# Attention of a two-layer encoder step: pairs alternate between kinds, transposed blocks are copied first, forget sums stand mid-column, units follow the last column piece

## The reference

```python
q_a, k_a, v_a, logf, q_b, k_b, v_b = _project(a, w_in[l], b_f[l], qn_a[l], kn_a[l], qn_b[l], kn_b[l])
F = jnp.cumsum(logf, axis=1)
y_a = _fox_attention(q_a, k_a, v_a, F, F, pos_p, pos_p)        # score + F[q] - F[k], causal, softmax
y_b = _swa_prompt(q_b, k_b, v_b, sink_l, slopes)               # banded, distance penalty, a sink in the softmax
h_p = _merge(h_p, y_a, y_b, w_out[l])
h_p = _channel(h_p, l, g_ffn, w_gate, w_up, w_down, w_router, b_router, we_gate, we_up, we_down)
```

## Time and profile before

| | us |
|---|---|
| median of 3 runs (1336.8 to 1343.54) | 1336.99 |
| the profiled execution | 1331.89 |
| its span | 1330.1 |
| PE busy in the span | 1244.0 (94%) |
| DVE busy | 845.2 (64%) |
| ACT busy | 645.8 (49%) |
| POOL busy | 262.4 (20%) |
| mean granted TensorE clock | 0.904 of full |

### The profile page before, as it was taken

How to read it: one execution, slowest core, us unless ns; L and a number is a source line. 1 busy time by engine, 2 the same in 40 slices (tenths; PEclk the granted TensorE clock), 3 DMA queues, 4 the chain that set the end, 5 groups by cost and what they waited for, 6 DMA issues and landing times.

```text
span 1330.1 us, 20704 instructions
## 1 busy us (share of the span) xinstructions
PE 1244.0 (94%) x7482; PEld 1101.7 (83%) x7482; DVE 845.2 (64%) x1232; ACT 645.8 (49%) x1051; POOL 262.4 (20%) x272
## 2 busy tenths in 40 slices
PE   6998999999999998999997888996999999999993
PEld 6995555579999998999995444886999999999993
DVE  5597444337555654343488553354988988988884
ACT  4533433324232332232433543344788788888871
POOL 3333232212000000111343432120012012012000
PEclk9997556579999998999998987897999999999997
DMA  6541014213333343332531034155999999999984
GB/s 252 209 129 37 1 44 154 102 35 111 126 127 114 123 140 113 117 118 87 212 124 51 1 128 169 51 197 171 363 382 353 378 386 350 379 383 359 370 321 153
DMA packets 58320, 246.72 MB, mean 185 GB/s; under 512 B 7390, under 2 KB 11054, under 8 KB 56208
## 3 DMA queue, kind: packets, MB, share of 16 engines
q1 hardware_dynamic: 53200, 232.78, 48.4%
q0 software_dynamic: 4192, 11.52, 2.3%
q10 hardware_dynamic: 864, 1.57, 0.3%
HBM read 235.22 MB, written 11.68 MB: 186 GB/s over the span
## 4 chain that ended last, share of the span: by engine, by line
PE 81%; ACT 5%; DVE 5%; DMA 4%; issue 3%; POOL 1%; SPq 0%; ACTq 0%; POOLq 0%; DVEq 0%
PE bank L707 21%; PE bank L709 21%; PE bank L708 21%; PE bank L805 4%; PE bank L784 3%; ACT WH L451 3%; PE bank L752 3%; DMA nf_pmt<-nf_rows 2%; DVE WL L457 2%; PE bank L820 2%; PE bank L772 1%; PE bank L768 1%; PE bank L866 1%; PE bank L814 1%; DVE rs L1356 1%
## 5 line engine op out<-in xcount | busy, mean ns | idle before, releaser
L457 DVE TENSOR_TENSOR WL<-raw,WH 128x1024 fp32r<-128x1024 f32 (+3 forms) x206 | 300.0, 1456 | 157.6 <-ACT WH L451 154.9
L451 ACT ACTIVATE WH<-raw 128x1024 fp32r<-128x1024 f32 (+3 forms) x206 | 254.3, 1234 | 286.8 <-PE bank L709 285.7
L707 PE MATMUL bank<-aH,WH 128*128 128x400 f32 (+1 forms) x688 | 246.4, 358 | 3.8 <-DVE aL L1452 1.9
L708 PE MATMUL bank<-aL,WH 128*128 128x400 f32 (+1 forms) x688 | 238.8, 347 | 0.0
L709 PE MATMUL bank<-aH,WL 128*128 128x400 f32 (+1 forms) x688 | 238.6, 347 | 0.0
L707 PE MATMUL bank<-WH,xTH 128*128 128x352 f32 x512 | 168.6, 329 | 3.8 <-DVE WL L457 1.9
L457 DVE TENSOR_TENSOR WL<-raw_more,WH 128x1408 fp32r<-128x1408 f32 (+2 forms) x96 | 156.5, 1644 | 22.4 <-ACT WH L451 21.4
L709 PE MATMUL bank<-WH,xTL 128*128 128x352 f32 x512 | 165.9, 324 | 0.0
L708 PE MATMUL bank<-WL,xTH 128*128 128x352 f32 x512 | 165.8, 324 | 0.0
L451 ACT ACTIVATE WH<-raw_more 128x1408 fp32r<-128x1408 f32 (+2 forms) x96 | 133.6, 1401 | 30.2 <-PE bank L709 29.5
L707 PEld LDWEIGHTS bank<-aH,WH 128*128 128x128 f32 x688 | 130.5, 190 | 9.0 <-DVE aL L1452 2.5
(11 more groups left out here) (208 smaller groups left out, 2099.6 us busy)
## 6 DMA issues: line engine op xcount, KB each, us to landing
raw<-w_egu SPq DMA_DIRECT2D x64, 704.0 KB, 5.9
raw_more<-w_egu SPq DMA_DIRECT2D x64, 704.0 KB, 6.1
raw<-w_gu SPq DMA_DIRECT2D x44, 512.0 KB, 3.5
raw_more<-w_ed SPq DMA_DIRECT2D x24, 768.0 KB, 6.1
raw<-w_ed SPq DMA_DIRECT2D x24, 640.0 KB, 6.6
raw<-w_col SPq DMA_DIRECT2D x26, 512.0 KB, 3.8
raw<-w_d SPq DMA_DIRECT2D x16, 704.0 KB, 4.1
kc<-ck_fox SPq DMA_DIRECT2D x8, 1024.0 KB, 7.4
```

The lines of the kernel that those rows point to most:

```text
L451: nc.scalar.activation(WH[:, p % SPL, 0:w], landing(p), ACT.Copy).then_inc(hi_ready, 1)
L457: nc.vector.tensor_tensor(WL[:, p % SPL, 0:w], landing(p), WH[:, p % SPL, 0:w].bitcast(F32), ALU.subtract).then_inc(lo_ready, 1)
L707: mm(out, aw[0], bw[0], start=start, stop=False)
L708: mm(out, aw[0], bw[1], start=False, stop=False)
```

## The change

Seven things change together:

- `unit_plan` takes the pair as the outer loop and the kind as the inner one: swa 0, fox 0, swa 1, fox 1, and so on. `pair_tile` and the waits of SP's loads follow.
- `COLS` is `[8, 9, 0, 4, 10, 1, 5, 11, 2, 6, 12, 3, 7]`: the swa key and query of pair 0 come first, the fox query and key of pair 3 last.
- The forget sums are formed after piece `XNF` = 4, DVE copies them behind column 4, and SP stores them after it has issued piece 9. The small term moves to the end of `prob`.
- Units follow the last piece: PE scores units 0 and 1 before the last head mean, units 2 and 3 as the banks of the last two roots come free, and the first transpose waits for all columns. ACT takes the last root, and DVE the last column, at step 2.
- POOL handles the last two columns after it has scaled unit 3.
- ACT does `copy_T(i-4)` ahead of `exps(i)`, and copies whole 128-key blocks in one instruction, the left-over one too.
- Scores go to banks 6, 2, 5 and 4 in turn.

```diff
-        for kind in ("swa", "fox"):
-            for pr in range(NPAIR):
+        for pr in range(NPAIR):
+            for kind in ("swa", "fox"):
...
-        eps_ms = nf_smp[:, :, :].rearrange("p s k -> p (s k)")[:, 0:T]
+        eps_ms = prob[:, :, :].rearrange("p n k -> p (n k)")[:, 4 * 384 - T:]
...
+                    if x == XNF + 5:
+                        sp.wait_ge(nf_copied, 2 * l + 2)
+                        sp.dma_start(nf_rows[l], NFp[l][0:H, :]).then_inc(nf_stored, 16)
+                        sp.dma_start(nf_seqs[l], NFs[l][0:64, :]).then_inc(nf_stored, 16)
...
+                for j, u in enumerate(BY_LAYER[l]):
+                    if j == 4:
+                        pool.wait_ge(norm_ready, u["n"])
+                        finish(NCOL - 2)
+                        finish(NCOL - 1)
+                        pool.wait_ge(qbd_ready, 8 * (l + 1))
...
+                    if x == XNF:
+                        pe.wait_ge(em_ready, l + 1)
+                        forget_sums()
...
-                pe.wait_ge(nf_copied, 2 * (l + 1))
-                pe.wait_ge(col_done, (l + 1) * NCOL)
                 for i in range(NU + LAG + 1):
+                    if i == 0:
+                        pe.wait_ge(nf_copied, 2 * (l + 1))
+                    elif i == 1:
+                        pe.wait_ge(col_done, l * NCOL + NCOL - 2)
+                    elif i in (2, 3):
+                        pe.wait_ge(colroot_ready, l * NCOL + NCOL - 3 + i)
+                    elif i == LAG:
+                        pe.wait_ge(col_done, (l + 1) * NCOL)
                     if i < NU:
                         scores(units[i])
+                    if i == 1:
+                        head_mean(NCOL - 1)
...
                 for i in range(NU + LAG + 2):
+                    if i == 2:
+                        head_root(NCOL - 1)
+                    if LAG <= i < NU + LAG:
+                        copy_T(units[i - LAG])
                     if i < NU:
                         exps(units[i])
-                    if LAG <= i < NU + LAG:
-                        copy_T(units[i - LAG])
...
+                    if i == 2:
+                        column(NCOL - 1)
                     if new:
                         add_bias(new)
```

More of the change, by code:

```diff
@@ L191 @@
 NCOL = NPAIR * 3 + 1
-COLS = [0, 4, 1, 5, 2, 6, 3, 7, 8, 9, 10, 11, 12]
+COLS = [8, 9, 0, 4, 10, 1, 5, 11, 2, 6, 12, 3, 7]
+XNF = 4
 CBODY = 6
@@ L620, in add_eps, with finish @@
                     nc.gpsimd.tensor_tensor(sq[:, i % 2, :], sq[:, i % 2, :], eps_ms, ALU.add).then_inc(sqe_ready, 1)
-                add_eps(0)
-                add_eps(1)
-                for x, c in enumerate(COLS):
-                    if x + 2 < NCOL:
-                        if x and (COLS[x - 1] < 4 or COLS[x - 1] > 8):
-                            pool.wait_ge(qbd_ready, 8 * l + sum(y < 4 or y > 8 for y in COLS[:x]))
-                        add_eps(x + 2)
-                    pool.wait_ge(sqe_ready, l * NCOL + min(x + 3, NCOL))
+                def finish(x):
+                    c = COLS[x]
                     pool.wait_ge(col_done, l * NCOL + x + 1)
@@ L642, in _ @@
                         pool.dma_start(o_kswa[l], qk[l][:, c, :]).then_inc(out_done, 16)
-                pool.wait_ge(qbd_ready, 8 * (l + 1))
-                for u in BY_LAYER[l]:
+                add_eps(0)
+                add_eps(1)
+                for x, c in enumerate(COLS):
+                    if x + 2 < NCOL:
+                        if x and (COLS[x - 1] < 4 or COLS[x - 1] > 8):
+                            pool.wait_ge(qbd_ready, 8 * l + sum(y < 4 or y > 8 for y in COLS[:x]))
+                        add_eps(x + 2)
+                    pool.wait_ge(sqe_ready, l * NCOL + min(x + 3, NCOL))
+                    if x < NCOL - 2:
+                        finish(x)
+                pool.wait_ge(sqe_ready, (l + 1) * NCOL)
+                pool.wait_ge(qbd_ready, 8 * l + sum(y < 4 or y > 8 for y in COLS[:-2]))
+                for j, u in enumerate(BY_LAYER[l]):
[4 more added lines that the diff above has]
+                        pool.wait_ge(qbd_ready, 8 * (l + 1))
                     n, rows, keys = u["n"], u["rows"], u["keys"]
@@ L766, in scores @@
                         pe.wait_ge(swc_loaded, 32 * (l + 1))
-                    pe.wait_ge(qbd_ready, l * 8 + d + 1)
+                    pe.wait_ge(qbd_ready, l * 8 + sum(c < 4 or c > 8 for c in COLS[:COLS.index(qc) + 1]))
                     mm(S[:, past:past + P], qbd[l][:, d, 128 * s:128 * s + 128], qk[l][:, kk, TP:T], start=True, stop=True)
@@ L856, in _, with forget_sums @@
                     last.then_inc(piece_done, 1)
+                def forget_sums():
+                    pe.wait_ge(logf_ready, l + 1)
+                    pe.wait_ge(va_copied, 4 * (l + 1))
+                    for i, (t0, r) in enumerate(QT[:3]):
+                        last = mm(bank[6][0:H, 0:TP], lf[0:r, i, :], negtri[0:r, TRI - t0:TRI - t0 + TP], start=(i == 0), stop=(i == 2))
+                    last.then_inc(nf_done, 1)
+                    pe.wait_ge(clf_loaded, 16 * (l + 1))
+                    pe.wait_ge(lbd_ready, l + 1)
+                    for c in range(2):
+                        mm(bank[7][0:64, 0:PAST], clf_sb[l][:, c, :], negtri[:, TRI - P * c:TRI - P * c + PAST], start=(c == 0), stop=(c == 1))
+                    for c in range(2):
+                        mm(bank[7][0:64, PAST:384], clf_sb[l][:, c, :], negones, start=(c == 0), stop=False)
+                    mm(bank[7][0:64, PAST:384], lbd[l][:, :], newtri, start=False, stop=True).then_inc(nf_done, 1)
                 def head_mean(x):
@@ L1154, in copy_T @@
                     PT = bank[7 if n % 2 else 3]
-                    nk = (keys - NMETA if keys % P else keys) // P
-                    if nk:
-                        last = A(probT[:, n % 3, 0:nk * P].rearrange("p (i w) -> p i w", i=nk)[:, :, 0:rows],
-                                 PT[:, 0:nk * P].rearrange("p (i w) -> p i w", i=nk)[:, :, 0:rows], ACT.Copy)
-                    if keys % P:
-                        w = keys % P
-                        last = A(probT[0:w, n % 3, nk * P:nk * P + rows], PT[0:w, nk * P:nk * P + rows], ACT.Copy)
+                    if keys < P:
+                        last = A(probT[0:keys, n % 3, 0:rows], PT[0:keys, 0:rows], ACT.Copy)
+                    else:
+                        w = -(-keys // P) * P
+                        last = A(probT[:, n % 3, 0:w], PT[:, 0:w], ACT.Copy)
                     last.then_inc(probT_copied, 1)
@@ L1345, in _, with column @@
                                 ALU.mult).then_inc(lbd_ready, 1)
-                for x in range(-1, NCOL):
+                def column(x):
                     if x + 1 < NCOL:
@@ L1361, in _ @@
                                            ALU.mult, ALU.mult).then_inc(col_done, 1)
-                dve.wait_ge(nf_done, 2 * l + 1)
-                V.tensor_copy(NFp[l][0:H, :], bank[6][0:H, 0:TP]).then_inc(nf_copied, 1)
-                dve.wait_ge(nf_done, 2 * l + 2)
-                V.tensor_copy(NFs[l][0:64, :], bank[7][0:64, 0:384]).then_inc(nf_copied, 1)
+                for x in range(-1, NCOL - 1):
+                    column(x)
+                    if x == XNF:
+                        dve.wait_ge(nf_done, 2 * l + 1)
+                        V.tensor_copy(NFp[l][0:H, :], bank[6][0:H, 0:TP]).then_inc(nf_copied, 1)
+                        dve.wait_ge(nf_done, 2 * l + 2)
+                        V.tensor_copy(NFs[l][0:64, :], bank[7][0:64, 0:384]).then_inc(nf_copied, 1)
                 if l == 0:
```

29 lines of the change are left out of this document (7 added, 22 removed).

## The result

The changed kernel took **1290.01 us** (median of 1284.22, 1290.01 and 2269.73; a fourth execution took 1306.77) against 1336.99 before, a ratio of 0.9612 with a 95% interval of 0.9529 to 0.9695. Its four executions there differ by 57 us, and the mean granted clock goes with them: 1257.39 us at 0.961, 1266.01 at 0.950, 1291.69 at 0.931 and 1314.43 at 0.908.

The account below looks back on a forecast made before the run. TensorE was taken as the bound, at half clock in layer 0's attention, with nf_pmt fetch and copy waits in layer 1. From 1331.9: 2 x 3.6 + 6.0 - 19.4 - 4.5 = -10.7, so 1321 us; range 1285 to 1336.

Parts of the forecast that it names:

- the rival: Layer 0's attention gets the full clock and keeps it for part: 1281 to 1315 us, chance 0.33.
- 3.3 us of forget sums per layer: Attention entry: forget sums behind column 4 lie on PE's path, no longer hidden behind DVE's reciprocals: +3.3 us.
- first transpose 15.9 behind the last piece: Attention entry: summed waits put the first transpose at 15.9 us instead of 15.6, 0.3 later against the last piece.
- the drain of 1.38 us: ScalarE's table switch at the entry: by the skill page 1.4 us later per layer, forecast 1324; left out.
- twice 3.6: Entry in both layers: forget sums 3.3 plus first transpose 0.3 later, +3.6 us per layer.
- -19.4 for alternating: Layer 1's fox pairs: nf_pmt's fetch hides behind the swa pair between, 14.4 plus 5 us saved.
- -4.5 for the copy: Layer 1's full-clock swa stretch: three quarters of PE's 6.0 us of waits for ScalarE's copies go.
- 12.21 + 12.75: Layer 1 at full clock: counted periods in us of one swa pair and one fox pair.
- In layer 0 at half clock PE doesn't wait, so nothing: Layer 0's attention: copy first gains nothing, as PE has no waits there.
- that spell came once in 160 us, and I don't count on it again: +6.0 us: Layer 0's attention: the profiled full-clock spell, three fox periods in 60.4 us instead of 66.4, is not expected again.
- Its price per two pairs: Layer 0 at full clock: 11.3 us less for each swa and fox pair, giving 1298 from mid-layer, 1281 from the first boundary.

Follow-up runs that it names:

- alt_fill: Kernel before with pairs alternating and PE's idle entry filled with matmuls nobody reads, copy still behind the newest exp in two instructions: 1298.62 us, ratio 0.9667.

## Why the prediction was right, and where it was not

The sign and the range held: 1290.01 lies between 1285 and 1336, though the second median, 1278.85, lies under it. The forecast itself, 1321 with layer 0 at half clock, did not come; it was missed by 31 and 42 us. That the first median fell into the range is owed to the rival's case, which the range took in for the most part, and in part to luck, since executions of this kernel spread over 57 us. Of the changed kernel's seven executions named here without the 2269.73, none reached the forecast's 1316 to 1329, five fall in the rival's 1281 to 1315, that layer 0 gets the full clock for part, and two lie under it.

**The entry: right to a quarter of a microsecond.** Predicted 3.3 us of forget sums per layer, measured 3.4 (the square behind them comes 8.46 us after the one ahead, 70.56 to 79.02, where others stand 5.04 apart). Predicted first transpose 15.9 behind the last piece, measured 15.67 in layer 0 and 15.92 in layer 1, by the steps named: a load of 1.28 and a root between two exps. The next activation stands 1.30 behind the load's start, so the drain of 1.38 us that the Trainium skill ("ScalarE: Activation LUTs", What ACT_TABLE_LOAD costs) adds to each load shows no more here than in the row that was preferred to it. The change's new entry is a loss by itself: 6.0 us with the clock held, where twice 3.6 was forecast.

**Layer 1: the sum 5.5 us short, the split wrong.** Predicted -19.4 for alternating and -4.5 for the copy, -23.9 together; measured 115.4 to 86.0, -29.4. Alone, in their profiled executions, they gave -10.4 and -14.4. The copy's term was mis-sized: I priced its 6.0 us of waits in the swa stretch, as their own length. With the fetch gone all four fox pairs run at full clock too, and a fox and a swa pair take 22.29 us, where 12.21 + 12.75 were counted: 2.7 us in each of four such pairs of pairs, 10.7, at full clock alone. And alternating was priced as if the fetch's were the only wait that drops the clock; in alternating alone it fell at 753 behind waits for copies. "In layer 0 at half clock PE doesn't wait, so nothing" was the second half of the same mistake: the row was right, but whether the full clock can be kept depends on it (alternating with the filled entry fell at 158 us, with the copy first it never did).

**Layer 0: the step that failed** is "that spell came once in 160 us, and I don't count on it again: +6.0 us". Measured -49.5 in the profiled execution (146.1 to 96.6). It is the shortest of the four; the other three have no trace. The spell was counted as an event of fixed length, when the trace of before had the wait that ended it. These are a row of the chain and the row of PE's timeline at the fall:

```profile
205.55 6.01 DMA nf_pmt<-nf_rows
```

```profile
213.37 1.23 PE L805 MATMUL bank<-probT,v_tok 128*64 128x128 f32 x4 [1.05 <-ACT probT L1161]
```

The fetch lands at 211.56, the copy behind it keeps PE waiting, and the clock falls at 213.5. The rival said so, and the sum gave it nothing. With the fetch and the copies off the path the clock, once risen, stays. When it rises varies, 153 us in one execution of the changed kernel and 270 in one of alternating with copy first. Between those two traces layer 0's attention differs by 51 us (96.6 and 147.6), which is the size of the 57 between the changed kernel's executions. Where it rises late, the forecast's picture holds, but its loss is less: 147.6 us instead of 146.1 in alternating with copy first, +1.5.

**The rival was named with its evidence, and priced too low.** Its price per two pairs was 11.3 us, from 40.4 at half clock and 29.1 at full clock, the latter layer 1's pairs times 7/6 for the seventh unit. Measured at full clock in layer 0: 23.28, so 17.1 per two pairs. Layer 1's 22.29 at full clock is within 1.0 us of that: the seventh unit, the meta unit, costs far less than the sixth that was added for it, and what copy first saves is in the rest.

**After layer 0** a few microseconds came that no term had: from the last transposition of sample rows to layer 1's last square it is 437.4 us against 438.7, though the columns within it grew by 3.4. The output projection meets a clock that is low for some 3 us, from 231 on; before, it ran at 0.50 until 285.

The steps add up, for the profiled executions: -49.5 - 29.4 - 4.7 for this stretch without the columns, + 6.8 for the columns, and + 2.4 for what lies before the first column, at the entries and after layer 1 give -74.4, and the spans differ by 1330.1 - 1255.6 = 74.5.

**What stays open.** What raises the clock in a busy layer 0 was not settled: it stood at 0.50 through 125, 142 and 157 us of an all but gapless PE, and rose at 153 us elsewhere. In the six traces in which it rose within layer 0's attention (at 153, 203, 223, 231, 255 and 270 us) it did so among or right behind the score or value matmuls of fox sample units, but most such stretches passed without a rise. In the kernel before the first of them comes at 187 us, in the changed kernel at 136: alternating may also bring the clock sooner, and no run isolates this. Nor was it settled how much waiting drops the clock: layer 1 before held 1.00 for 54.5 us with 6.0 us of waits, layer 0 of alternating with the filled entry lost it after 33 us with 4.7 us idle.

## What to carry to other kernels

Where a stage runs at half clock with TensorE fully busy, ask first which idle time took the clock and which waits would take it again: the price of such a wait is not its length but all that follows at half speed until the clock is back (1.07 us ahead of 104 at half clock in alt_fill); not every such wait takes it. Removing one of several such waits shows little, and so does restoring the clock while one is left; here the fetch (by alternating), the copy's place and the filled entry gave 38, 18 and 7 us one at a time and 98 us together, by the medians. Matmuls that nobody reads, in time that was idle anyway, kept the clock through the entry and also took the spread out of the times.

## What the hardware showed that was not expected

- A TensorE busy for 125.00 of 125 us stayed at a granted clock of 0.50 (alternating alone, 126 to 251). The Trainium skill ("TensorE: Matmul & The Clock Gate", What's actually happening) says that activity releases the throttle; by the rows here a busy engine is not enough, and what else it takes was not found.
- Executions of the same kernel on one chip spread over 57 us, and the mean granted clock went with them (1257.39 at 0.961, 1314.43 at 0.908). With its entry filled the kernel spread over 8.6 us, and alternating and copy first with the entry filled over 2.83.
